# Queries and keys moved in two parts by Pool and SP, two products for each differential map, and the bias in two transfers: a two-layer encoder on one NeuronCore

## The chip, the core and the metric

The kernel runs on one core of one Trainium2 chip. The metric is the device time of one execution in microseconds (us). The kernel before takes 1178.91 us, the median of 3 runs (1178.65 to 1179.13).

## The reference, cut to what matters

The input x is 256 tokens by 2048, float32. Two layers follow each other; each is a norm, one input projection, attention in several head groups, a gate, one output projection, a norm and the residual.

```python
# layer 0: w_in is 2048 x 8192
h = rms_norm(x, pre_g)
qa, ka, va, ga, qb, kb, vb, gb = split(h @ w_in)
oa = neighbourhood_attention(qa, ka, va, rpb)   # 8 heads of 128, bias by distance in row and column
# B: 8 heads, each with two maps over 64 of the 128 rows of q and k
qb = partial_rope(qb.reshape(b, s, 8, 2, 64)); kb = partial_rope(kb.reshape(b, s, 8, 2, 64))
sc = einsum("bqhcd,bkhcd->bchqk", qb, kb) * 64 ** -0.5
p = softmax(sc)
ob = einsum("bhqk,bkhd->bqhd", p[:, 0] - lam * p[:, 1], vb)
x = x + rms_norm(concat(oa * silu(ga), rms_norm(ob) * 0.8 * silu(gb)) @ w_out, post_g)
# layer 1: w_in is 2048 x 12288: three dilated windows (8 heads each), merged by their
# denominators, and 8 query heads over 2 key heads with a sink; then the same gate, w_out and norm
```

## The kernel before, in words

**Every weight is used once**, so the kernel streams 196 chunks of 1 MB (four blocks of 128 rows by 512 columns). SP loads chunk n into one of 4 raw buffers (L354), ACT rounds it to float32r (`w_hi`, L760), DVE subtracts to get the rest (`w_lo`, L1054), and TensorE makes three products for each pair of block and token tile: hi by hi, lo by hi, hi by lo (L497). That is 24 products of 128 rows by 512 columns for a chunk. ACT and DVE prepare chunk s + 2 while TensorE is at chunk s; there are 3 split buffers.

**A body** is 12 chunks: four give 512 columns of queries (blk 0), four the keys (blk 1), four the values (blk 2). ACT takes a finished block out of PSUM into `unit` (L767), Pool applies the rotary turn to queries and keys (`rotate`, L440 to L447; none for kind A). The attention of a body's four heads (a unit) is worked into the next body: each engine's program calls `attention(u, h)` for the half chunks h = 0 to 23, `h = 2 s` and `2 s + 1`, in its own fixed order. The order on DVE in slot s is: `attention(2s)`, `attention(2s+1)`, the transposition of the next unit's queries and keys if s is 10 (`turn_qk`, L1096, two instructions), then `split_lo` for chunk s + 2. For kind D `attention(2s+1)` comes after `split_lo`. ACT has `attention(2s)`, `split_hi`, `attention(2s+1)`.

**Queries and keys need the head dimension on the partitions.** DVE transposes blocks of 32 x 32 into `postg` (`blocks`); then SP issues 16 moves of 64 KB (`gather`, L361), each with the query and the key part of one 32-partition group, into `qk_raw`. SP's queue carries the weight loads too, and the moves stand ahead of the load of the same slot. ACT and DVE split the result into hi and lo for kinds A, W, B and D (`split_qk_hi` at h = 2, `split_qk_lo` at h = 3).

**The units** are, in order: A, A, B, B in layer 0; W, W, G, G, G, G, D in layer 1. Layer 0 has 5 bodies, layer 1 has 8. Kind B are the differential heads. Its queries are split into `split_q`, where map 0 has rows 0 to 63 and map 1 rows 64 to 127, and Pool has set the other half to zero (L464); the keys are `k_hi` and `k_lo` over all 128 rows. A map of a head is then three products of 128 rows by 256 keys for each of two tiles (L629):

```python
for t in range(NT):
    for n, (a, b) in enumerate(PARTS):   # hi*hi, hi*lo, lo*hi
        m = nc.tensor.matmul(..., split_q[:, c, a, t * UH + j, :],
                             keys_of((k_hi[:, :, :], k_lo)[b], j), start=(n == 0), stop=(n == len(PARTS) - 1))
```

Kind D transposes its shared keys on TensorE at h = 4 (`turn_shared_k`, L580), after Pool's rotary turn of the third block, which is in the same slot as ACT's taking of it.

**The bias of kind A** is loaded by Pool in 32 transfers of 64 KB (L422) into `mix`, two for each head and tile, as runs of 64 elements; DVE adds the mask in the last four slots of the first body (L1452), one semaphore for each pair of heads.

Of the kernel before, what the change touches and what calls it, by code (L numbers as in the profile page):

```python
# [27 lines left out]
P = 128  # L28
# [16 lines left out]
TURN = 10  # L45
QK_DMAS = 16 * QUADS * QUADS
# [5 lines left out]
RPB_R, RPB_C = 15, 31  # L52
SCALE = HEAD ** -0.5
# [6 lines left out]
CREDITED = ("o_full", "o_taken", "probs_turned", "pt_ready", "probs_ready", "unit_done", "o_squared", "roped")  # L60
# [78 lines left out]
def build(nc, weights, x_turned, x_perm, consts, identity, pre_g, post_g, rpb, lam, subln, sink, out):  # L139
    with ExitStack() as ctx:  # L140
# [14 lines left out]
        with nc.sbuf_tensor("split_q", [P, 2, 2, NT * UH, P], F32R) as split_q:  # L155
            pass
# [28 lines left out]
        with nc.sbuf_tensor("q_lo", [P, 2, NT * UH, P], F32R) as q_lo:  # L185
# [16 lines left out]
        warm = sb("warm", [P, 1])  # L202
        std = sb("std", [P, NT])
# [33 lines left out]
        blocks = postg[:, :].rearrange("p (j b n) -> p j b n", j=QUADS, b=2)  # L237

        acc = [[ctx.enter_context(nc.psum_tensor(f"acc{s}_{t}", [P, NB], F32)) for t in range(NT)]
               for s in range(3)]  # L240
# [4 lines left out]
                 "x_hi first_hi first_lo warm_in ones_in row_sums row_full hi_ready lo_ready chunk_used tile_done proj_ready roped rope_a "  # L245
                 "mix_turned sp_moved1 sp_moved0 pool_moved1 pool_moved0 turn_full turn_hi turn_taken qk_turned qk_in qk_hi qk_ready k_full k_split k_ready g_ready "
# [4 lines left out]
                 "pre_sq pre_sum pre_var pre_std pre_rdy lam_p lam_s lam_e bias_rdy "  # L251
                 "y_sq y_scaled y_sum y_var y_std y_rdy "
                 "rs_v rs_s rs_rdy tanh_done gate_u gate_done q_zeroed").split()
# [6 lines left out]
        bias_in_two = [sem(f"bias_in_two{i}") for i in range(UH)]  # L260
# [47 lines left out]

        def split_units(u):

            return u.index - 4 if u.kind == "D" else u.index
# [19 lines left out]
        def _(sp):  # L331
# [44 lines left out]
            for layer in range(2):  # L376
# [3 lines left out]
                for u, b, i in loops(sp, layer):  # L380
                    for s in range(BODY):
                        if u is not None and u.by_blocks:
                            for h in (2 * s, 2 * s + 1):
                                for j in u.stages(h, 2):
                                    move_probs(u, j)
                        if s == TURN and turned_next(layer, u) is not None:
                            gather(turned_next(layer, u))
                        load(CHUNK0[layer] + BODY * b + s + 2 + RAW, i)
# [14 lines left out]
        def _(pool):  # L403
# [11 lines left out]
            for h in range(8):  # L415
                for t in range(NT):
                    for half in range(2):
                        r = 2 * t + half
                        src = bass.AP(rpb.tensor, h * RPB_R * RPB_C + (7 - r) * RPB_C + 15 - (GRID_W - 1),
                                      [[1, GRID_W], [RPB_C, ROWS], [1, GRID_W]])  # L420
                        at = (h * NT + t) * SEQ
                        pool.dma_start(bias_in[half * 64:half * 64 + 64, at:at + SEQ].rearrange(  # L422
                            "p (j k) -> p j k", j=ROWS), src).then_inc(bias_in_two[h // 2], 16)
# [24 lines left out]

            pool.wait_ge(S["consts_in"], 16)
            for layer in range(2):  # L450
                for u, _, _ in loops(pool, layer):
                    if u is None or u.kind == "A":
                        continue
                    turns = ((0, NB), (1, NB), (2, 2 * HEAD)) if u.kind == "D" else ((0, NB), (1, NB))
                    for k, (blk, cols) in enumerate(turns):
# [5 lines left out]
                    if layer == 0 and u.index == 2:  # L461

                        pool.wait_ge(S["masked"], 2 * UH)
                        pool.memset(split_q[:, :, :, :, :].rearrange("p c b a n -> p (c b a n)").bitcast(F32), 0.0).then_inc(  # L464
                            S["q_zeroed"], 1)
                if layer == 0:

                    pool.wait_ge(S["qk_in"], QK_DMAS * UNITS[0])
# [13 lines left out]
        def _(pe):  # L482
# [268 lines left out]
        def _(act):  # L751
# [49 lines left out]
            def split_qk_hi(u):  # L801

                act.wait_ge(S["qk_in"], QK_DMAS * u.index + QK_DMAS)
                if u.kind == "B":

                    act.wait_ge(S["q_zeroed"], 1)
# [11 lines left out]
                else:  # L818
                    nc.scalar.activation(k_hi[:, :, :], qk_raw[:, :, 1, :], ACT.Copy).then_inc(S["qk_hi"], 1)
# [11 lines left out]
            def attention(u, h):  # L831
# [5 lines left out]
                if h == 2:  # L837
                    split_qk_hi(u)
                if h == 4 and u.kind == "D":
# [105 lines left out]
            for layer in range(2):  # L945
# [4 lines left out]
                for u, b, i in loops(act, layer):  # L950
                    for s in range(BODY):
# [3 lines left out]
                        if s in takes:  # L955
# [7 lines left out]
                            if u is not None and s > 0:  # L963

                                act.wait_ge(S["qk_turned"], u.index + 1)
# [82 lines left out]
        def _(dve):  # L1048
# [39 lines left out]
            def turn_qk(layer, index):  # L1088

                if layer == 0 and index < 2:  # L1090

                    dve.wait_ge(S["proj_ready"], PROJ0[0] + 3 * index + 2)
                else:
                    dve.wait_ge(S["roped"], CREDIT + 2 * (index - 2) + 2)
                for blk in range(2):
                    m = nc.vector.transpose(blocks[:, :, blk, :].rearrange("p j (n c) -> p j n c", c=QUAD),  # L1096
                                            unit[:, blk, :, :].rearrange("p t (h j c) -> p j (t h) c", j=QUADS, c=QUAD))
                m.then_inc(S["qk_turned"], 1)

            def split_qk_lo(u):  # L1100

                for blk in range(2):

                    dve.wait_ge(S["qk_hi"], 2 * split_units(u) + blk + 1)
                    if u.kind == "B" and blk == 0:
                        for c in range(2):
                            rows = slice(64 * c, 64 * c + 64)
                            m = nc.vector.tensor_tensor(by_quads(split_q[rows, c, 1, :, :]), raw_quads(0, rows),
                                                        by_quads(split_q[rows, c, 0, :, :].bitcast(F32)), ALU.subtract)
                    elif blk == 0 or u.kind == "D":  # L1110
# [150 lines left out]
            def attention(u, h):  # L1261
                if u is None:
                    return
                if h == 3 and u.kind != "G":
                    split_qk_lo(u)
                if h == 4 and u.kind == "D":
# [136 lines left out]
            for layer in range(2):  # L1403
# [5 lines left out]
                for u, b, i in loops(dve, layer):  # L1409
                    for s in range(BODY):  # L1410
# [25 lines left out]
                        if s == TURN and turned_next(layer, u) is not None:  # L1436
                            turn_qk(layer, turned_next(layer, u))
# [152 lines left out]
```

## Time and profile before

| | |
|---|---|
| median of 3 runs | 1178.91 us (1178.65 to 1179.13) |
| the profiled execution, device time | 1178.83 us |
| its span, first to last instruction | 1176.6 us |
| mean granted TensorE clock | 0.998 |
| TensorE products busy | 1163.8 us, 99% of the span, 5476 products |
| DVE, ACT, Pool busy | 736.4, 583.8, 121.0 us |
| moved by DMA | 245.23 MB, 208 GB/s in the mean |

The profiled execution takes 2.2 us more than its span, for what lies around the first and the last instruction. It is 0.08 us below the median. A product's own duration in the profile is modelled and overlaps with the next one, so its cost is read from the distance between starts, or from a chain of many products.

### The profile page before, as it was taken

Reading aid. Unit: us, or ns where it says so; the run is one execution under the profiler, and the core shown is the slowest. Engines: PE = TensorE matmul, PEld = TensorE weight load, DVE = VectorE, ACT = ScalarE, POOL = GpSimd, SP = SyncE. Lnnn points to the kernel's source line nnn. Section 1 sums busy time; section 2 is a strip of 40 time slices with the busy share of each in tenths; the row PEclk is TensorE's granted clock in tenths of the full one; section 3 lists DMA queues with packets and bytes.
Section 4 is the critical chain, followed back from the end, with each engine's and each line's share of the span. In section 5 each row is a group of like instructions: output and inputs, shape, how many; then the busy total and the mean of one; then the engine's idle time right before and its main releaser. Section 6 shows DMA issues by size and latency. Waiting matters only on the chain.

```text
span 1176.6 us, 14665 instructions
## 1 busy us (share of the span) xinstructions
PE 1163.8 (99%) x5476; PEld 972.6 (83%) x5476; DVE 736.4 (63%) x842; ACT 583.8 (50%) x745; POOL 121.0 (10%) x177
## 2 busy tenths in 40 slices
PE   8999999999999999999999999999999999999997
PEld 6888888888888888888888888888888888888886
DVE  6676566656764975764666555565746667668654
ACT  6554445544555654564545454445444444446442
POOL 2400002000000310010100101102011002002100
PEclk9999999999999999999999999999999999999999
DMA  9987666744646785455767666666765766455741
GB/s 355 242 238 251 215 227 211 232 170 152 249 148 248 176 267 184 153 205 179 248 209 228 220 201 230 207 222 197 253 201 170 249 188 228 143 182 179 258 152 72
DMA packets 86441, 245.23 MB, mean 208 GB/s; under 512 B 33729, under 2 KB 51521, under 8 KB 60913
## 3 DMA queue, kind: packets, MB, share of 16 engines
q1 hardware_dynamic: 82704, 235.44, 60.2%
q0 software_dynamic: 3392, 8.96, 2.9%
q8 instruction: 36, 0.59, 0.2%
q14 instruction: 21, 0.16, 0.0%
q10 hardware_dynamic: 288, 0.08, 0.0%
HBM read 221.37 MB, written 8.39 MB: 195 GB/s over the span
## 4 chain that ended last, share of the span: by engine, by line
PE 96%; DVE 2%; ACT 1%; DMA 1%; issue 0%; SPq 0%; DVEq 0%; ACTq 0%
PE acc L497 89%; PE bank_x L660 2%; PE bank_y L613 1%; DMA raw<-weights 1%; PE bank_x L656 1%; PE bank_y L602 1%; PE bank_x L644 1%; DVE w_lo L1054 1%; PE bank_y L629 0%; PE bank_x L629 0%; PE bank_y L609 0%; DVE mix L1310 0%; ACT w_hi L760 0%; DVE resid L1365 0%; DVE probs L1301 0%
## 5 line engine op out<-in xcount | busy, mean ns | idle before, releaser
L497 PE MATMUL acc<-w_hi,act_hi 128*128 128x512 f32 x1560 | 615.8, 395 | 3.8 <-DVE w_lo L1054 3.8
L497 PE MATMUL acc<-w_lo,act_hi 128*128 128x512 f32 x1560 | 608.7, 390 | 0.0
L1054 DVE TENSOR_TENSOR w_lo<-raw,w_hi 128x2048 fp32r<-128x2048 f32 x195 | 449.0, 2305 | 180.6 <-ACT w_hi L760 180.4
L760 ACT ACTIVATE w_hi<-raw 128x2048 fp32r<-128x2048 f32 x195 | 373.5, 1916 | 298.7 <-PE acc L497 282.3
L497 PE MATMUL acc<-w_hi,act_lo 128*128 128x512 f32 x1560 | 418.2, 390 | 0.0
L497 PEld LDWEIGHTS acc<-w_hi,act_hi 128*128 128x128 f32 x1560 | 293.4, 188 | 62.1 <-issue 3.5
L497 PEld LDWEIGHTS acc<-w_hi,act_lo 128*128 128x128 f32 x1560 | 293.3, 188 | 62.2 <-DVE act_lo L1072 0.4
L497 PEld LDWEIGHTS acc<-w_lo,act_hi 128*128 128x128 f32 x1560 | 293.5, 188 | 57.3
L767 ACT ACTIVATE unit<-acc,pre_r 128x512 f32<-128x512 f32 x78 | 49.4, 685 | 123.0 <-PE acc L497 119.8
L440 POOL TENSOR_TENSOR rope_c<-unit,cst 128x256 f32<-128x256 f32 (+1 forms) x19 | 14.1, 740 | 728.0 <-ACT unit L767 596.2
L1213 DVE TENSOR_SCALAR mix<-bank_x 128x256 f32<-128x256 f32 (+1 forms) x24 | 10.1, 421 | 65.8 <-PE bank_x L660 65.8
L782 ACT ACTIVATE probs<-scores,negm 128x256 f32<-128x256 f32 (+1 forms) x80 | 36.4, 458 | 29.7 <-DVE negm L1142 25.3
L1213 DVE TENSOR_SCALAR unit_out<-bank_x 128x256 f32<-128x256 f32 x16 | 6.8, 424 | 60.7 <-PE bank_x L656 60.7
L660 PEld LDWEIGHTS bank_x<-unit,pT 128*128 128x128 f32 x256 | 33.5, 191 | 2.5
L447 POOL TENSOR_TENSOR unit<-rope_c,rope_s 128x256 f32<-128x256 f32 (+1 forms) x19 | 34.9, 1838 | 1.5
L326 POOL DMA_DIRECT2D mix_raw<-mix_blocks x48 | 25.6, 541 | 84.0 <-DVE mix_blocks L1321 83.8
L660 PE MATMUL bank_x<-unit,pT 128*128 128x128 f32 x256 | 33.7, 274 | 0.0
L1096 DVE STREAM_TRANSPOSE postg<-unit 128x1024 f32<-128x1024 f32 x22 | 26.0, 1219 | 0.0
L991 ACT ACTIVATE probs<-acc 128x512 f32<-128x512 f32 x16 | 9.5, 595 | 32.5 <-PE acc L497 32.5
L1139 DVE TENSOR_REDUCE rmax<-scores 128x2 f32<-128x512 f32 (+1 forms) x40 | 23.2, 580 | 1.4
L1337 DVE TENSOR_TENSOR mix<-acc,postg 128x512 f32<-128x512 f32 x16 | 10.5, 687 | 19.6 <-ACT probs L991 19.6
L827 ACT ACTIVATE pT<-probs 128x512 f32<-128x512 f32 (+1 forms) x32 | 16.6, 518 | 9.7 <-DMA probs<-p_moved 9.6
(179 smaller groups left out, 619.6 us busy)
## 6 DMA issues: line engine op xcount, KB each, us to landing
raw<-weights SPq DMA_DIRECT2D x195, 1024.0 KB, 5.0
qk_raw<-postg SPq DMA_DIRECT2D x176, 64.0 KB, 2.1
p_moved<-p_blocks SPq DMA_DIRECT2D x16, 256.0 KB, 5.5
probs<-p_moved SPq DMA_DIRECT2D x64, 64.0 KB, 1.9
mix<-rpb POOLq DMA_DIRECT2D x32, 64.0 KB, 22.4
postg<-post_g POOLq DMA_DIRECT2D x2, 1024.0 KB, 8.0
resid<-x_perm POOLq DMA_DIRECT2D x2, 1024.0 KB, 8.6
p_moved<-p_blocks SPq DMA_DIRECT2D x16, 128.0 KB, 5.0
```

The source lines that it names most:

```text
L326: eng.dma_start(dst, mix_blocks[a * QUAD:(a + 1) * QUAD, c % 2, q, :, :, :]).then_inc(S[f"{done}{c % 2}"], 16)
L447: pool.tensor_tensor(v[whole], rc, rs, ALU.add).then_inc(S["roped"], 1)
L497: m = nc.tensor.matmul(tiles[t][:, :], a[:, kt, t * P:(t + 1) * P], w[:, buf, kk * NB:(kk + 1) * NB], start=(kt == 0 and a is act_hi and w ...
L660: m = nc.tensor.matmul(X[:, t * P:(t + 1) * P], pT[:, (t * NT + k) * P:(t * NT + k + 1) * P], unit[:, 2, k, col:col + HEAD], start=(k == 0 ...
L760: nc.scalar.activation(w_hi[:, at % SPLIT, :], raw[:, at % RAW, :], ACT.Copy).then_inc(S["hi_ready"], 1)
L767: m = nc.scalar.activation(dst[:, t, :], acc[blk][t][:, :], ACT.Copy, scale=pre_r[:, t:t + 1])
L782: m = nc.scalar.activation(probs[:, j % 2, t * w:(t + 1) * w], scores[:, j % 2, t * w:(t + 1) * w], ACT.Exp, bias=negm[:, 2 * j + t:2 * j ...
L827: nc.scalar.activation(pT[:, 0:n * P].rearrange("p (n a c) -> p a n c", a=QUADS, c=QUAD), probs[:, j % 2, 0:n * P].rearrange("p (a n c) -> ...
L1054: nc.vector.tensor_tensor(w_lo[:, at % SPLIT, :], raw[:, at % RAW, :], w_hi[:, at % SPLIT, :].bitcast(F32), ALU.subtract).then_inc(S["lo_r ...
L1096: m = nc.vector.transpose(blocks[:, :, blk, :].rearrange("p j (n c) -> p j n c", c=QUAD), unit[:, blk, :, :].rearrange("p t (h j c) -> p j ...
L1139: nc.vector.reduce_max(rmax[:, two], dst.rearrange("p (t n) -> p t n", t=NT), AX_X).then_inc(S["maxed"], 1)
L1213: nc.vector.tensor_scalar(dst, src, 1.0, None, ALU.mult).then_inc(S["o_taken"], 1)
```

## The change

Five edits go together.

- The queries of the next unit are transposed by DVE at slot 6 and the keys at slot 10 (8 and 10 in a layer's first body), one instruction each. Pool moves the queries in 16 DMAs of 32 KB as soon as they are transposed, and half of the keys in 8; SP moves the other half in 8. Before each group Pool does one sum of a column (`tick`).
- A differential map is two products for each tile. For map c the stationary operand holds the hi part of the queries in its own 64 rows and the lo part in the other 64; the moving operand `both_k[:, c, 0]` holds the hi part of the keys in both halves. One product of 128 rows is then hi*hi plus lo*hi. The second, hi*lo, is over the map's own 64 rows only (rows 0 to 63 for map 0, 64 to 127 for map 1).
- For this ACT makes six copies of 64 rows for a B unit, and DVE four differences of 64 rows; the semaphore is counted per map. Pool's filling with zeros is gone.
- The bias comes in two DMAs with runs of 219 elements; the DVE sum reads it through a strided, reversed access pattern.
- ACT's splitting of B and D is called at h = 1 and no longer at h = 2; DVE's for B at h = 2 and 3, for D at h = 2; D's transposition of the shared keys on TensorE, and what follows it on ACT and DVE, at h = 3.

```diff
-TURN = 10
-QK_DMAS = 16 * QUADS * QUADS
+TURNS = (6, 10)
+FIRST_TURNS = (8, 10)
+PART_DMAS = 16 * QUADS * QUADS
+HALF_DMAS = PART_DMAS // 2
...
-            def gather(index):
-
-                sp.wait_ge(S["qk_turned"], index + 1)
-                for a in range(QUADS):
+            def gather_keys(index):
+
+                sp.wait_ge(S["k_turned"], index + 1)
+                for a in (0, 1):
                     for j in range(QUADS):
-                        sp.dma_start(qk_raw[j * QUAD:(j + 1) * QUAD, a, :, :], blocks[a * QUAD:(a + 1) * QUAD, j, :, :]).then_inc(
-                            S["qk_in"], 16)
+                        sp.dma_start(qk_raw[j * QUAD:(j + 1) * QUAD, a, 1, :], blocks[1][a * QUAD:(a + 1) * QUAD, j, :]).then_inc(
+                            S["k_in_sp"], 16)
...
-            for h in range(8):
-                for t in range(NT):
-                    for half in range(2):
-                        r = 2 * t + half
-                        src = bass.AP(rpb.tensor, h * RPB_R * RPB_C + (7 - r) * RPB_C + 15 - (GRID_W - 1),
-                                      [[1, GRID_W], [RPB_C, ROWS], [1, GRID_W]])
...
+            for half in range(2):
+
+                src = bass.AP(rpb.tensor, (7 - 2 - half) * RPB_C + 15 - (GRID_W - 1),
+                              [[1, GRID_W], [RPB_R * RPB_C, 8], [1, BIAS_RUN]])
+                pool.dma_start(bias_in[half * 64:half * 64 + 64, 0:8 * BIAS_RUN].rearrange("p (h n) -> p h n", h=8),
+                               src).then_inc(S["bias_in"], 16)
...
+            def gather(index, blk):
+
+                pool.wait_ge(S[("q", "k")[blk] + "_turned"], index + 1)
+                pool.wait_ge(S["ticked"], CREDIT + 2 * index + blk)
+                pool.tensor_tensor(tick[:, :], cst[:, 0:1], cst[:, 1:2], ALU.add).then_inc(S["ticked"], 1)
+                for a in (range(QUADS), (2, 3))[blk]:
+                    for j in range(QUADS):
+                        pool.dma_start(qk_raw[j * QUAD:(j + 1) * QUAD, a, blk, :], blocks[blk][a * QUAD:(a + 1) * QUAD, j, :]).then_inc(
+                            S[("q", "k")[blk] + "_in"], 16)
...
-                    if layer == 0 and u.index == 2:
-
-                        pool.wait_ge(S["masked"], 2 * UH)
-                        pool.memset(split_q[:, :, :, :, :].rearrange("p c b a n -> p (c b a n)").bitcast(F32), 0.0).then_inc(
-                            S["q_zeroed"], 1)
+                        if blk < 2:
+                            gather(u.index, blk)
...
             def score_map(u, j, c):
+                pe.wait_ge(S["qk_ready"], 2 * split_units(u) + c + 1)
                 if c == 0:
-                    pe.wait_ge(S["qk_ready"], 2 * split_units(u) + 2)
...
                 for t in range(NT):
-                    for n, (a, b) in enumerate(PARTS):
+                    for part, rows in enumerate((slice(0, P), slice(64 * c, 64 * c + 64))):
                         m = nc.tensor.matmul((Y, X)[c][:, t * SEQ:(t + 1) * SEQ].rearrange("p (t a c) -> p t a c", t=NT, a=QUADS),
-                                             split_q[:, c, a, t * UH + j, :],
-                                             keys_of((k_hi[:, :, :], k_lo)[b], j), start=(n == 0), stop=(n == len(PARTS) - 1))
+                                             q_hi[rows, c, t * UH + j, :], keys_of(both_k[rows, c, part, :, :], j),
+                                             start=(part == 0), stop=(part == 1))
...
-                if u.kind == "D" and h == 4:
+                if u.kind == "D" and h == 3:
                     turn_shared_k(u)
...
             def split_qk_hi(u):
...
                     for c in range(2):
-                        rows = slice(64 * c, 64 * c + 64)
-                        m = nc.scalar.activation(by_quads(split_q[rows, c, 0, :, :]), raw_quads(0, rows), ACT.Copy)
-                    m.then_inc(S["qk_hi"], 1)
+                        mine, other = (slice(64 * r, 64 * r + 64) for r in (c, 1 - c))
+                        nc.scalar.activation(by_quads(q_hi[mine, c, :, :]), raw_quads(0, mine), ACT.Copy).then_inc(S["qk_hi"], 1)
+                        nc.scalar.activation(both_k[other, c, 0, :, :], qk_raw[mine, :, 1, :], ACT.Copy)
+                        nc.scalar.activation(both_k[mine, c, 0, :, :], qk_raw[mine, :, 1, :], ACT.Copy).then_inc(S["qk_hi"], 1)
+                    return
...
+            def split_both_lo(u, c):
+
+                mine, other = (slice(64 * r, 64 * r + 64) for r in (c, 1 - c))
+                dve.wait_ge(S["qk_hi"], hi_count(u) + 2 * c + 1)
+                nc.vector.tensor_tensor(by_quads(q_hi[other, c, :, :]), raw_quads(0, mine),
+                                        by_quads(q_hi[mine, c, :, :].bitcast(F32)), ALU.subtract)
+                dve.wait_ge(S["qk_hi"], hi_count(u) + 2 * c + 2)
+                nc.vector.tensor_tensor(both_k[mine, c, 1, :, :], qk_raw[mine, :, 1, :],
+                                        both_k[mine, c, 0, :, :].bitcast(F32), ALU.subtract).then_inc(S["qk_ready"], 1)
...
-                if h == 3 and u.kind != "G":
+                if u.kind == "B" and h in (2, 3):
+                    split_both_lo(u, h - 2)
+                if h == (2 if u.kind == "D" else 3) and u.kind not in ("B", "G"):
                     split_qk_lo(u)
```

## Rows read from the trace of the kernel before

**Rows 1.** The page: busy time of the engines, and the chain that ended last.

```profile
PE 1163.8 (99%) x5476; PEld 972.6 (83%) x5476; DVE 736.4 (63%) x842; ACT 583.8 (50%) x745; POOL 121.0 (10%) x177
PE 96%; DVE 2%; ACT 1%; DMA 1%; issue 0%; SPq 0%; DVEq 0%; ACTq 0%
```

**Rows 2.** Waits of TensorE: line, releaser, us in total, times, longest.

```profile
PE acc L497 <- DVE w_lo L1054: 3.8, 2, 3.1
PE bank_x L539 <- DVE pT L1390: 1.1, 1, 1.1
```

**Rows 3.** Products of L629 into bank y with the low keys: duration min/median/max, first and last start.

```profile
L629 PE MATMUL bank_y<-qk_low,split_q x16: 282/283/290, 236.7 to 355.1; 128*128 128x256 f32 x16
```

**Rows 4.** The chain in order of time, four of its pieces: start us, us.

```profile
236.73 0.72 PE bank_y L629 x6
...
249.63 0.89 PE bank_x L660 x8
...
251.24 2.73 PE acc L497 x12
...
330.75 0.72 PE bank_x L629 x6
```

**Rows 5.** Timeline of TensorE at two places: start us, us [idle before].

```profile
249.47 1.05 PE L660 MATMUL bank_x<-unit,pT 128*128 128x128 f32 x8
250.27 0.37 PE L629 MATMUL bank_y<-k_hi,split_q 128*128 128x256 f32 x1
250.48 0.28 PE L629 MATMUL bank_y<-qk_low,split_q 128*128 128x256 f32 x1
...
392.88 1.07 PE L497 MATMUL acc<-w_hi,act_lo 128*128 128x512 f32 x4
394.59 0.50 PE L497 MATMUL acc<-w_hi,act_hi 128*128 128x512 f32 x1 [0.64 <-DVE w_lo L1054]
394.93 0.39 PE L497 MATMUL acc<-w_lo,act_hi 128*128 128x512 f32 x1
```

**Rows 6.** DMA instructions by line: duration on the issuing queue, ns min/median/max.

```profile
L326 POOL DMA_DIRECT2D mix_raw<-mix_blocks x48: 496/550/622, 392.7 to 1097.6; - x48
DMA to landing us min/median/max: 1.7/4.9/6.6
...
L361 SPq DMA_DIRECT2D qk_raw<-postg x176: 507/591/1352, 72.6 to 977.5; - x176
L422 POOL DMA_DIRECT2D mix<-rpb x32: 622/692/770, 23.8 to 42.7; - x32
```

**Rows 7.** Timeline of ACT, DVE, TensorE around the second B unit's splitting.

```profile
292.88 2.36 DVE L1096 STREAM_TRANSPOSE postg<-unit 128x1024 f32<-128x1024 f32 x2
301.18 1.91 ACT L760 ACTIVATE w_hi<-raw 128x2048 fp32r<-128x2048 f32 x1
306.72 2.14 ACT L809 ACTIVATE split_q<-qk_raw 64x1024 fp32r<-64x1024 f32 x2 [3.63 <-DMA qk_raw<-postg]
309.85 3.71 ACT L760 ACTIVATE w_hi<-raw 128x2048 fp32r<-128x2048 f32 x2
312.52 2.28 DVE L1054 TENSOR_TENSOR w_lo<-raw,w_hi 128x2048 fp32r<-128x2048 f32 x1
317.57 0.40 PE L497 MATMUL acc<-w_hi,act_hi 128*128 128x512 f32 x1
```

**Rows 8.** Timeline of Pool, DVE and TensorE at the start of unit D.

```profile
979.97 2.37 POOL L443 TENSOR_TENSOR rope_s<-unit,cst 128x64 f32<-128x64 f32 x1
982.42 2.39 POOL L447 TENSOR_TENSOR unit<-rope_c,rope_s 128x128 f32<-128x128 f32 x1
979.75 7.21 DVE L1054 TENSOR_TENSOR w_lo<-raw,w_hi 128x2048 fp32r<-128x2048 f32 x3
985.19 0.39 PE L497 MATMUL acc<-w_hi,act_hi 128*128 128x512 f32 x1
```

**Rows 9.** Timeline of DVE in the first body: the first sum of the bias.

```profile
64.02 1.42 DVE L1452 TENSOR_TENSOR resid<-mix,cst 128x256 f32<-128x256 f32 x4
```

More of the change, by code:

```diff
@@ L154, in build @@
         mix = sb("mix", [P, NT, D_MODEL])
-        with nc.sbuf_tensor("split_q", [P, 2, 2, NT * UH, P], F32R) as split_q:
+        with nc.sbuf_tensor("both_k", [P, 2, 2, QUADS, NT * UH * QUAD], F32R) as both_k:
             pass
@@ L202, in build @@
         warm = sb("warm", [P, 1])
+        tick = sb("tick", [P, 1])
         std = sb("std", [P, NT])
@@ L259, in build @@
         landed = [sem(f"landed{i}") for i in range(RAW)]
-        bias_in_two = [sem(f"bias_in_two{i}") for i in range(UH)]
         def const(name):
@@ L307, in in_token_order, with hi_count @@
             return src, dst[:, c * CK + k, :].rearrange("p (n b r) -> p n b r", n=4, b=4)
+        def hi_count(u):
+            return 2 * split_units(u) + (0 if u.kind == "A" else 2 * (u.index - 2) if u.kind == "B" else 4)
         def split_units(u):
@@ L385, in _ @@
                                     move_probs(u, j)
-                        if s == TURN and turned_next(layer, u) is not None:
-                            gather(turned_next(layer, u))
+                        if s == TURNS[1] and turned_next(layer, u) is not None:
+                            gather_keys(turned_next(layer, u))
                         load(CHUNK0[layer] + BODY * b + s + 2 + RAW, i)
@@ L836, in attention @@
                         order_pT(u, j)
-                if h == 2:
+                if h == (1 if u.kind in ("B", "D") else 2):
                     split_qk_hi(u)
-                if h == 4 and u.kind == "D":
+                if h == 3 and u.kind == "D":
                     act.wait_ge(S["k_full"], 1)
@@ L1100, in split_qk_lo @@
[L1100 to L1110, printed above, removed]
+                    dve.wait_ge(S["roped"], CREDIT + 2 * (index - 2) + 1 + blk)
@@ new lines, in turn_part @@
+                nc.vector.transpose(blocks[blk][:, :, :].rearrange("p j (n c) -> p j n c", c=QUAD),
+                                    unit[:, blk, :, :].rearrange("p t (h j c) -> p j (t h) c", j=QUADS, c=QUAD)).then_inc(
+                    S[("q", "k")[blk] + "_turned"], 1)
+            def split_both_lo(u, c):
[6 more added lines that the diff above has]
+                                        both_k[mine, c, 0, :, :].bitcast(F32), ALU.subtract).then_inc(S["qk_ready"], 1)
@@ L1111, in split_qk_lo @@
+            def split_qk_lo(u):
+                dve.wait_ge(S["k_in"], HALF_DMAS * u.index + HALF_DMAS)
+                dve.wait_ge(S["k_in_sp"], HALF_DMAS * u.index + HALF_DMAS)
+                for blk in range(2):
+                    dve.wait_ge(S["qk_hi"], hi_count(u) + blk + 1)
+                    if blk == 0 or u.kind == "D":
                         m = nc.vector.tensor_tensor(by_quads(q_lo[:, blk, :, :]), raw_quads(blk),
@@ L1263, in attention @@
                     return
-                if h == 3 and u.kind != "G":
+                if u.kind == "B" and h in (2, 3):
+                    split_both_lo(u, h - 2)
+                if h == (2 if u.kind == "D" else 3) and u.kind not in ("B", "G"):
                     split_qk_lo(u)
-                if h == 4 and u.kind == "D":
+                if h == 3 and u.kind == "D":
                     dve.wait_ge(S["k_split"], 1)
@@ L1435, in _ @@
                             turned(16 * layer + 2 * s + 2, layer)
-                        if s == TURN and turned_next(layer, u) is not None:
-                            turn_qk(layer, turned_next(layer, u))
+                        at = FIRST_TURNS if u is None else TURNS
+                        if s in at and turned_next(layer, u) is not None:
+                            turn_part(layer, turned_next(layer, u), at.index(s))
                         split_lo(CHUNK0[layer] + BODY * b + s + 2, i)
```

58 lines of the change are left out of this document (32 added, 26 removed).

## The prediction

> **What bounds the kernel now.** I read the page first: products fill 99% of the span, and the chain that ended last runs for 96% through TensorE [rows 1]. Then the waits of TensorE: it stood for 3.8 us behind `w_lo` (3.1 us of it near the start, 0.64 us at 394.59 us), and for 1.1 us behind its very first operand [rows 2, 5]. So nothing in the middle is late but one chunk. What is saved on ACT, DVE, Pool or a queue is worth nothing while this holds; what is saved on TensorE is worth all of it, as long as `w_lo` still comes in time.
>
> A product's own duration (0.283 us for a differential one [rows 3]) is no price, since products overlap. The chain gives the price: 6 differential products of a map take 0.72 us, at its first map as at its last, 0.120 us each [rows 4]. There are 8 heads of two maps, 16 maps, 96 products, 11.5 us.
>
> **The change part by part.**
>
> *Two products for three.* A map has 4 products in place of 6. The two that go are of the same shape as the rest: 2 x 0.120 = 0.24 us a map, 16 x 0.24 = 3.84 us in all. All of it is on the path.
>
> *The product over 64 rows.* No row of before shows one. At the low end it takes nothing, being hidden in its neighbour: 32 more slots of 0.120 us, another 3.84 us gained. At the high end TensorE stands empty each time it goes between 128 and 64 rows. Within a map the order is 128, 64, 128, 64 and then 128 again, 4 transitions a map, 64 in all. The price of an empty engine is in the trace. After 392.88 us four products follow each other and the next should start 4 x 0.227 = 0.91 us later (twelve take 2.73 us [rows 4]), at 393.79; its operand was late, and it started at 394.59, then took 0.34 us to its successor and not 0.227 us [rows 5]. The first product's surplus of 0.11 us is what a start on an empty array costs. To run empty costs what a product is in flight beyond its slot, 0.283 - 0.120 = 0.163 us [rows 3, 4]. Together 0.27 us a transition at the worst, 64 x 0.27 = 17.5 us. The nearest rows are other changes of the kind of product. Eight value products of 128 columns in full float32 stand between float32r products. From 249.47 us they and the first differential product take 1.01 us until 250.48 [rows 5]; eight at 0.111 us (0.89 us in the chain [rows 4]) and one at 0.120 us make 1.01 us. Changing the kind is free within the 0.01 us the trace resolves. I take 0.006 us a transition, half of that, 0.4 us in all, and a full slot of 0.120 us for the product over 64 rows, since its 256 columns are the same and I know of no row in which fewer rows shorten it.
>
> The Trainium skill (TensorEngine Tiling, Key Properties) speaks against this: changing the tiling mode, and not just the tile, drains TensorE, and it counts 64 rows as a mode of its own. By the Trainium skill (TensorE: Matmul & The Clock Gate, Part 2, step 4) a drain is some 128 cycles, an estimate of 0.053 us at 2.4 GHz; 64 of them are 3.4 us, and the sum would be 1178.4 us.
>
> *Splitting on ACT and DVE.* For a B unit ACT had 3 copies and now has 6, each 1.07 us whether over 64 rows or 128 [rows 7], 3.2 us more, twice. They stand at the same place of its order as before (nothing lies between h = 1 and h = 2 there). DVE goes from 3 to 4 differences of some 1.2 us. Neither is on the path; the cover is the lead of `w_lo`. In the second B unit it is thinnest: `w_lo` of the fourth chunk was done at 312.52 + 2.28 = 314.80 us and TensorE wanted it at 317.57 us, 2.8 us of lead [rows 7]. ACT had then waited 3.6 us for the moves.
>
> *The moves.* In that unit DVE could transpose only at 292.88 us [rows 7]. Now the queries are long gone by then (slot 6) and the keys need one instruction, to 294.1 us. Pool's `tick` may be held by DVE's `w_lo`: beside DVE's row of three, two of Pool's small sums ran 2.37 and 2.39 us and ended with DVE's instructions [rows 8]. That is up to 296.4 us. Eight DMAs of 0.55 us on Pool end at 300.8 us; landing takes 4.9 us, at the most 6.6 us [rows 6]: 305.7 to 307.4 us. SP's eight at 0.59 us are out by 299 us, 4.7 us earlier than its 16 were, so the weight loads behind them gain. ACT is free at 303.1 us, so its wait is 2.6 to 4.3 us; six copies end at 312.1 to 313.8 us, `w_hi` 1.9 us and `w_lo` 2.3 us later, 316.3 to 318.0 us. Against 317.57 us this is a lead of 1.3 us or a stall of 0.4 us. I take no stall. Elsewhere Pool has 16 x 0.55 = 8.8 us for the queries between slots 6 and 8 (two slots are 11 us), and SP is relieved; the other thin place, the chunk at 394.59 us [rows 5], hangs on the end of the last head and moves along with TensorE. DVE's two transpositions are only apart, not more.
>
> *D's shared keys* move from h = 4 to h = 3, that is to the half chunk that starts at 985.19 us. Pool's rotary turn ends at 982.42 + 2.39 = 984.81 us [rows 8], so 0.4 us are left. Nothing is gained by coming earlier. If Pool slips by one of DVE's instructions, TensorE stands up to 2 us.
>
> *The bias, the zeros.* 32 DMAs of 0.69 us become two with fewer, longer runs; the first use is at 64.02 us, the issue was over by 43.4 us [rows 6, 9]. Pool's filling goes too. Pool and DMA have room in both places and TensorE waits for neither: 0. It costs nothing while both transfers land in the 39 us from 25 to 64 us; DVE now needs both at once.
>
> **The sum**, against the profiled execution's 1178.83 us (span 1176.6 and 2.2 us around it): 1178.83 - 3.84 + 0.4 = 1175.4 us. That execution is 0.08 us under the median of the three runs, which I leave in the rounding. A change of over 0.2% (2.4 us) is about what a measurement can tell from none, so the forecast, -0.3%, is little beyond it.
>
> **The rivals.**
>
> *A, the forecast:* a transition costs up to 0.02 us; 1175.0 to 1176.4 us. For it: changing the kind of product is free [rows 5]. Against it: those all use the full height of the array.
>
> *B, a part of the gain is given back:* each transition costs 0.02 to 0.10 us, because the array empties in part. The break-even is 3.84 / 64 = 0.060 us. Middle: 64 x 0.055 = 3.5 us, 1178.5 us, no change that can be told. The drain that the Trainium skill (TensorEngine Tiling, Key Properties) names falls in here.
>
> *C, slower:* at each transition within `score_map` TensorE waits for the whole product in flight, 0.163 us or more, since the next weights can't be loaded under it. 64 x 0.163 = 10.4 us, 1185.4 us; with the surplus of an empty start 1192.5 us. It decides from 0.10 us a transition (6.2 us less 3.8 us is 2.4 us). For it: the row at 394.59 us shows that an emptied TensorE pays. Against it: there it had waited for data, not for itself.
>
> *D, late keys:* in the second B unit or at D's shared keys TensorE stands 0.4 to 2 us: 1175.8 to 1177.4 us. For it: leads of 1.3 and 0.4 us. Against: both hold by the rows.
>
> *E, the 64-row product is hidden in part:* down to 1171.5 us. Both products write the same sums one after the other, so I give it little.
>
> **How the numbers follow.** A 0.49, B 0.24, C 0.18, D 0.06, E 0.03. Faster by over 0.2% is A, E and a third of D, with rounding 0.53; within it B and the rest of D, 0.28; slower C and a little of B, 0.19. Predicted: 1175.4 us. A's own range is 1174.5 to 1176.4 us. The range reaches from 1174.5 us, where E begins and the spread of runs (0.25 us) is taken in, through B, whose end is 1181.2 us, to 1182.0 us; C's bulk and E are left out.
>
> **What would show it.** Right: 64 differential products, a map of four taking 0.48 us in the chain, the one over 64 rows with a start distance near 0.120 us, and the big product behind a map at its usual distance. The wait of TensorE for `w_lo` stays 3.8 us in total with no new line in its list; all 3.4 us are gained between 236 and 360 us and later stretches are as long as before. Wrong by B or C: distances of 0.14 us and more around the 64-row product, a map of 0.55 us or more. Wrong by D: a wait of TensorE on `w_lo` near 317 us or on Pool's line 447 near 985 us. The prediction is wrong if the gain comes from any stretch without B heads, or from the start.

## The result, and the profile after

The changed kernel is slower: 1187.84 us, the median of four runs (1186.87 to 1188.27), against 1179.02 us of the kernel before beside it (1178.65 to 1180.33), a ratio of 1.0074, 95% interval 1.0062 to 1.0087. The prediction was 1175.4 us, faster, and its range ended at 1182.0 us. The profiled execution took 1187.74 us, with a span of 1185.9 us and a granted clock of 0.995 (before: 0.998).

The page after, busy time of the engines:

```profile
PE 1172.6 (99%) x5444; PEld 972.1 (82%) x5444; DVE 740.4 (62%) x844; ACT 590.4 (50%) x751; POOL 254.1 (21%) x433
```

TensorE still sets everything (the chain that ended last runs for 96% through it, as in [rows 1]), with 32 products fewer and 8.8 us more of busy time. Nearly all of the 9.3 us by which the span grew are time in which the page shows TensorE busy. Waits of TensorE in the kernel after (columns as in [rows 2]):

```profile
PE acc L513 <- DVE w_lo L1076: 4.6, 2, 4.0
```

This is the wait of before, 0.8 us longer. The others are there in both kernels: 1.1 us at the very start, on `w_hi` 0.5 us (0.8 us before) and on `resid` 0.3 us. No wait on keys and none on Pool's turn has come. So the loss isn't a wait for another engine. The chain after, columns as in [rows 4]:

```profile
237.52 1.06 PE bank_y L645 x4
238.58 2.92 PE acc L513 x12
...
367.08 1.06 PE bank_x L645 x4
```

Four differential products take 1.06 us where six took 0.72 us [rows 4], and the twelve big ones behind a map 2.92 us where twelve take 2.73 us. It is the same at the first head and at the last. The groups of TensorE after, one row for each shape (columns: busy us, mean ns of one | idle before):

```profile
L645 PE MATMUL bank_y<-both_k,q_hi 64*128 64x256 f32 x16 | 6.1, 383 | 0.0
L645 PE MATMUL bank_y<-both_k,q_hi 128*128 128x256 f32 x16 | 5.8, 364 | 0.0
L645 PE MATMUL bank_x<-both_k,q_hi 128*128 128x256 f32 x16 | 5.3, 334 | 0.0
```

The records of the products over half the rows are 0.1 us longer than that of a full one was (0.283 us, [rows 3]), and those of the full ones next to them 0.05 to 0.08 us longer. The place is narrow enough to see single starts. TensorE and its weight loads (PEld) at the first map after:

```profile
237.36 1.22 PE L645 MATMUL bank_y<-both_k,q_hi 128*128 128x256 f32 x4
238.51 0.50 PE L513 MATMUL acc<-w_hi,act_hi 128*128 128x512 f32 x1
238.85 0.39 PE L513 MATMUL acc<-w_lo,act_hi 128*128 128x512 f32 x1
```

```profile
237.14 0.19 PEld L645 LDWEIGHTS bank_y<-both_k,q_hi 128*128 128x128 f32 x1
237.57 0.81 PEld L645 LDWEIGHTS bank_y<-both_k,q_hi 64*128 64x128 f32 x3 [0.25 <-issue]
```

The first product of the map starts at 237.36 us. The load of the second one's weights, over 64 rows, starts only at 237.57 us, 0.21 us later, and PEld had stood for 0.25 us with nothing that the profile names to wait for. A slot of 256 columns is 0.120 us [rows 4], so the load starts 0.09 us after the slot was over, and 0.07 us before the (modelled) end of that product's record. The record of the second product begins together with its load and is 0.10 us longer than usual (0.383 us, above); the third follows 0.31 us behind it. So a change of height (a step, from here on) costs some 0.09 us in front of the first product of the new height and some 0.10 us behind its start. The starts in the map are 237.36, 237.57, 237.88 and 238.20 us, the big product's is 238.51 us: 0.21 us, then three times 0.31 us, and 0.34 us instead of 0.227 us to the second big one.

**Where the 9 us arose.** Counting by the starts of the weight chunks, the same chunk starts 0.79 us later than before at 24 us. Each head of B then adds 1.0 to 1.1 us (its two maps together), 8.6 us over the eight heads, and from 376 us to the end the difference stays at 9.4 us. TensorE in stretches (us, busy (instructions), granted clock, DMA share, GB/s), first before, then after:

```profile
236.00:376.00 140.00, 140.00 (x710) 1.00 0.54 195
376.00:1169.00 793.00, 792.10 (x3702) 1.00 0.61 200
```

```profile
236.00:385.00 149.00, 149.00 (x679) 1.00 0.51 182
385.00:1179.00 794.00, 793.10 (x3705) 1.00 0.61 200
```

710 products less the 32 removed are 678; after needs 149 us for 679. The granted clock is 1.00 in both, and the stretch behind it is equal to 1 us in 793.

### The profile page after: what moved, and what is told of

It is laid out like the page before. It is cut to its first block, busy times and chain, and to the rows that moved or that the text cites. A ratio compares the mean times of both kernels' runs of the same rounds, so it can differ in the third digit from the quotient of the medians.

```text
span 1185.9 us, 14840 instructions
## 1 busy us (share of the span) xinstructions
PE 1172.6 (99%) x5444; PEld 972.1 (82%) x5444; DVE 740.4 (62%) x844; ACT 590.4 (50%) x751; POOL 254.1 (21%) x433
## 4 chain that ended last, share of the span: by engine, by line
PE 96%; DVE 2%; ACT 1%; DMA 1%; issue 0%; SPq 0%; DVEq 0%; ACTq 0%
PE acc L513 88%; PE bank_x L676 2%; PE bank_y L629 1%; PE bank_y L645 1%; PE bank_x L645 1%; PE bank_x L672 1%; PE bank_y L618 1%; DMA raw<-weights 1%; PE bank_x L660 1%; DVE w_lo L1076 1%; PE bank_y L625 0%; DVE mix L1340 0%; ACT w_hi L776 0%; DVE resid L1395 0%; DVE probs L1331 0%
## 5 line engine op out<-in xcount | busy, mean ns | idle before, releaser
L460 POOL DMA_DIRECT2D qk_raw<-postg x264 | 130.5, 502 | 5.7 <-issue 5.7
L457 POOL TENSOR_TENSOR tick<-cst 128x1 f32<-128x1 f32 x22 | 25.2, 1146 | 266.2 <-DVE postg L1117 232.2
```

Source lines behind the costliest of these rows:

```text
L457: pool.tensor_tensor(tick[:, :], cst[:, 0:1], cst[:, 1:2], ALU.add).then_inc(S["ticked"], 1)
L460: pool.dma_start(qk_raw[j * QUAD:(j + 1) * QUAD, a, blk, :], blocks[blk][a * QUAD:(a + 1) * QUAD, j, :]).then_inc(S[("q", "k")[blk] + "_in ...
```

## The experiments

The first four kernels separate three theories. One: a step between 128 and 64 rows costs about 0.19 us, four times a map (the theory of the steps, T in the expectations). Two: a product over 64 rows is slow in itself, whatever its neighbours (of the rows, S). Three: the new moves and copies hold TensorE up (of the moves, R). Each kernel starts from the one after, unless it says otherwise.

**Both products over all rows.** The half of the second operand that map 0 doesn't use is zeroed once by Pool, and the product takes all 128 rows.

```
- enumerate((slice(0, P), slice(64 * c, 64 * c + 64)))
+ enumerate((slice(0, P), slice(0, P)))
+ pool.wait_ge(S["masked"], 2 * UH)
+ pool.wait_ge(S["ticked"], CREDIT + 2 * u.index + 2)
+ pool.memset(both_k[:, :, 1, :, :] ..., 0.0).then_inc(S["q_zeroed"], 1)
+ act.wait_ge(S["q_zeroed"], 1)
```

> The changed kernel, but the second product of a map over all 128 rows; Pool fills the other half of its keys with zeros once. Theory T (going between 128 and 64 rows costs TensorE some 0.19 us each time, and nothing else in the change costs): no transitions are left, each of the 64 differential products is 0.12 us apart, a map has 0.48 us in the chain, the time is 1175 to 1176.5 us. Rival R (the changed kernel loses by what else is in it: the moves by Pool, more copies on ACT, the start): the time stays at 1184 us or more.

Measured: 1176.1 us (1175.1 to 1177.19, 11 runs), ratio to before 0.9979 (0.997 to 0.9988). TensorE at the same map, and its weight loads:

```profile
237.03 0.64 PE L650 MATMUL bank_y<-both_k,q_hi 128*128 128x256 f32 x4
...
237.74 0.39 PE L518 MATMUL acc<-w_lo,act_hi 128*128 128x512 f32 x1
```

```profile
237.03 0.43 PEld L650 LDWEIGHTS bank_y<-both_k,q_hi 128*128 128x128 f32 x3
237.39 0.19 PEld L518 LDWEIGHTS acc<-w_hi,act_hi 128*128 128x128 f32 x1
```

Four products now take 0.48 us, 0.120 us each, and every weight load starts beside the product in flight. From the map's first product to the second big one behind it: 0.71 us, after 1.49 us. That is 0.78 us for 4 steps, 0.195 us each. The moves, copies and splits are all still those of the changed kernel, so the theory of the moves falls: they aren't what loses 9 us. They aren't quite free either, as "Where the gain of the full rows went" shows.

**The order 128, 128, 64, 64.** The two loops change places: two steps a map instead of four, the same products.

```
- for t ...: for part, rows in enumerate(...):
+ for part, rows in enumerate(...): for t ...:
+ start=(part == 0 and t == 0), stop=(part == 1 and t == NT - 1)
```

> The changed kernel, but a map's four products in the order 128, 128, 64, 64 rows: two transitions a map in place of four. Theory T (the price is on the transition, 0.19 us): 32 fewer, 6.2 us less, 1181.7 us, and between the two products over 64 rows the starts are 0.12 us apart. Rival S (the price is on every product over 64 rows, and on the one behind it by its weights): the distance after each of the two stays at 0.31 us and the time near 1187.8 us.

Measured: 1180.9 us (1179.81 to 1181.89, 10 runs), ratio 1.0019 (1.001 to 1.0028).

```profile
235.80 0.83 PE L645 MATMUL bank_y<-both_k,q_hi 128*128 128x256 f32 x4
...
236.90 0.40 PE L513 MATMUL acc<-w_lo,act_hi 128*128 128x512 f32 x1
```

1.10 us over the same distance, 0.39 us above the full rows for two steps: 0.195 us each. The number of 64-row products is the same as in the changed kernel; were the product slow in itself, 1.49 us would have stayed. One expectation failed: the two products over 64 rows start 0.22 us apart (236.13 and 236.35 us) and not 0.12 us, since the second half of the step into 64 rows is paid behind the first of them.

**Before, with all six products over the map's own 64 rows.** This has 96 short products and two steps a map, into the run and out of it. The other half of the rows held zeros before, so leaving it out changes no sum.

```
+ rows = slice(64 * c, 64 * c + 64)
- split_q[:, c, ...], keys_of((k_hi[:, :, :], k_lo)[b], j)
+ split_q[rows, c, ...], keys_of((k_hi[:, :, :], k_lo)[b][rows], j)
```

> The kernel before, but all six products of a map over the map's own 64 rows: 96 products over 64 rows, two transitions a map, 32 in all. Theory T: 32 x 0.19 = 6.2 us more than the kernel before, 1185.2 us, and 0.12 us between starts inside a map. Rival S (every product over 64 rows takes 0.31 us): 96 x 0.19 = 18.5 us more, 1197.5 us.

Measured: 1185.53 us (1184.82 to 1185.78, 4 runs), ratio 1.0057 (1.0042 to 1.0072).

```profile
236.97 0.39 PE L497 MATMUL acc<-w_hi,act_lo 128*128 128x512 f32 x1
237.29 0.39 PE L630 MATMUL bank_y<-k_hi,split_q 64*128 64x256 f32 x1
237.51 0.28 PE L630 MATMUL bank_y<-qk_low,split_q 64*128 64x256 f32 x1
237.63 0.40 PE L630 MATMUL bank_y<-k_hi,split_q 64*128 64x256 f32 x2
237.87 0.28 PE L630 MATMUL bank_y<-qk_low,split_q 64*128 64x256 f32 x1
237.99 0.28 PE L630 MATMUL bank_y<-k_hi,split_q 64*128 64x256 f32 x1
...
238.53 0.40 PE L497 MATMUL acc<-w_lo,act_hi 128*128 128x512 f32 x1
```

Inside the run the short products start 0.12 us apart (237.51, 237.63, 237.87, 237.99), like full ones. That decides against the theory of the rows: the product isn't slow, the step is. One can see both steps of the map: into 64 rows, the last product of the old height takes 0.32 us to its successor (0.227 us is usual for 512 columns) and the first of the new height 0.22 us to its own (0.12 us is usual), 0.19 us more together. Out of 64 rows the same two surpluses stand again. For comparison the same map in the kernel before:

```profile
236.57 0.28 PE L629 MATMUL bank_y<-k_hi,split_q 128*128 128x256 f32 x1
...
237.52 0.39 PE L497 MATMUL acc<-w_lo,act_hi 128*128 128x512 f32 x1
```

Counted from the start of the big product before the map, it is 0.95 + 0.227 = 1.18 us there against 238.53 - 236.97 = 1.56 us here: 0.38 us for two steps. So the price is paid into 64 rows and out again, and with 512-column products on the other side too.

**The 64-row product first.** Its order is 64, 128, 64, 128, still four steps, now with the first behind a product of 512 columns. If a long product hid the step's work, this would be faster.

```
- for part, rows in enumerate((slice(0, P), slice(64 * c, 64 * c + 64))):
+ for part, rows in ((1, slice(64 * c, 64 * c + 64)), (0, slice(0, P))):
+ start=(part == 1), stop=(part == 0)
```

> The changed kernel, but within each tile the product over 64 rows comes first: 64, 128, 64, 128. There are four transitions a map as before, but the first of them now follows a product of 512 columns and not one of 256. Theory T with a price that does not depend on the product before (it is the way through the array): 1187.8 us. If the price is the loading of weights that can't be hidden under a short product, the long one hides it and the map costs up to 0.19 us less, 16 x 0.19 = 3.1 us less, 1184.7 us.

Measured: 1186.61 us (1186.03 to 1187.39, 4 runs), ratio 1.007 (1.0055 to 1.0086). It is the changed kernel's time (1186.77 us in its repeat below). In the chain, TensorE from the map's first product:

```profile
236.11 1.26 PE bank_y L645 x4
237.38 2.72 PE acc L513 x12
```

The map takes 1.26 us and the twelve behind it 2.72 us, together 3.98 us as after (1.06 + 2.92 us). Only the place of the last 0.2 us has moved. Nothing is hidden under 512 columns.

Averaged over all 16 maps, from the start of the last product before a map (a big one, in 6 of the 16 a product with the values) to that of the second big one behind it, the six kernels give:

| kernel | steps a map | products | us | over the row with its products and no step, per step |
|---|---|---|---|---|
| before | 0 | 6 | 1.139 | |
| all 64 rows | 2 | 6 | 1.526 | 0.193 |
| full rows | 0 | 4 | 0.898 | |
| grouped | 2 | 4 | 1.284 | 0.193 |
| after | 4 | 4 | 1.674 | 0.194 |
| 64 first | 4 | 4 | 1.674 | 0.194 |

**Where the gain of the full rows went.** By that table the maps give back 16 x 0.241 = 3.85 us, just the 3.84 us of the prediction, but the medians differ by some 2.8 us (0.9979 of 1178.9 is 1176.4, and 1176.1 was measured). By chunk starts in the profile, TensorE is 2.71 us earlier behind the eight heads than ahead of them. Two places took 0.27 us (273 us) and 0.54 us (322 us) back, and 0.33 us lie in a few ns here and there on the products of 512 columns. DVE at the first of them, then TensorE at the second, full rows:

```profile
265.74 1.24 DVE L1123 STREAM_TRANSPOSE postg<-unit 128x1024 f32<-128x1024 f32 x1
266.90 2.25 DVE L1082 TENSOR_TENSOR w_lo<-raw,w_hi 128x2048 fp32r<-128x2048 f32 x1
269.07 0.68 DVE L1184 TENSOR_REDUCE bmax<-bank_x 128x2 f32<-128x512 f32 x1
```

```profile
322.02 0.66 PE L665 MATMUL bank_x<-ident,probs 128*128 128x128 f32 x4 [0.33 <-DVE probs L1208]
```

At the first, the transposition of the queries now stands ahead of a `w_lo` and pushes the row maximum of the second map back; with maps this short the softmax comes too late by a little. The second is the place where ACT makes its six copies. Whether the slots mattered was tried by moving the two turns (slots 6 and 10 in the changed kernel and with full rows). First 7 and 10, full rows otherwise:

```
- TURNS = (6, 10)
+ TURNS = (7, 10)
```

> The kernel with full-height products (e1), but the queries are transposed in slot 7 and no longer in slot 6. e1 gained 3.7 us on the maps and gave back 0.8 us at two heads: 0.27 us near 273 us (fourth slot pair of the first B unit) and 0.54 us near 322 us (first head of the second). Theory T2 (in slot 6 DVE's transposition and the split behind it stand between the two maps of head 2, and TensorE then waits for the probabilities): the first of the two goes, the second stays, 0.27 us less than e1 in the trace; that is at the edge of what the times can tell. Rival (that wait comes from Pool's DMAs or from the shorter maps alone): both stay.

Measured: 1175.25 us (1173.64 to 1176.98, 11 runs), ratio 0.9972 (0.9963 to 0.9981). In the profile the loss at 273 us is gone, as expected. One of 0.23 us at 284 us has come, where Pool's rotary turn now falls together with DVE's softmax (see the last section), and that near 320 us stays at 0.51 us.

Then 7 and 9:

```
- TURNS = (6, 10)
+ TURNS = (7, 9)
```

> As e5, and the keys are transposed in slot 9, ahead of the last head's output, so that their moves land some 5 us earlier. Theory T3 (the 0.54 us near 322 us come from the keys of the second B unit landing at 304 us, which makes ACT late for the first head): this wait goes too, 0.8 us less than e1 in the trace. Rival (DVE now waits in slot 9 for Pool, which is still issuing the queries' moves before its rotary turn of the keys, and w_lo gets late): a new wait of TensorE for w_lo, no gain or a loss in the units from the second on.

Measured: 1175.97 us (1174.19 to 1176.96, 11 runs), ratio 0.9976 (0.9967 to 0.9985). The wait at 322 us is gone, as the theory that it comes from late keys expected. ACT's first copy of the second B unit at full rows, then ACT and DVE in the kernel with 7 and 9:

```profile
304.36 1.06 ACT L833 ACTIVATE q_hi<-qk_raw 64x1024 fp32r<-64x1024 f32 x1 [2.31 <-issue]
```

```profile
302.37 1.05 ACT L833 ACTIVATE q_hi<-qk_raw 64x1024 fp32r<-64x1024 f32 x1
```

```profile
313.43 0.69 DVE L1184 TENSOR_REDUCE bmax<-bank_y 128x2 f32<-128x512 f32 x1 [0.36 <-PE bank_y L650]
```

At full rows ACT waits 2.31 us for the keys, its six copies end at 310.82 us, and DVE is busy without a gap from the `w_lo` behind them (312.79 us) to the row maximum of the second map. With the keys a slot earlier ACT waits for nothing, that `w_lo` starts at 310.78 us, and DVE has 0.36 us to spare before the first maximum. So the 0.54 us come from the keys' landing and the copies behind it, by way of the softmax. But new losses have come, 0.22 us at 286 us and 0.79 us at 290 us. DVE in this kernel, then TensorE:

```profile
283.61 1.03 DVE L1200 TENSOR_SCALAR scores<-scores,binv 128x256 f32<-128x256 f32 x2
284.73 1.24 DVE L1208 SCALAR_TENSOR_TENSOR probs<-scores,bw 128x256 f32<-128x256 f32 x2
285.90 1.23 DVE L1123 STREAM_TRANSPOSE postg<-unit 128x1024 f32<-128x1024 f32 x1
287.06 2.25 DVE L1082 TENSOR_TENSOR w_lo<-raw,w_hi 128x2048 fp32r<-128x2048 f32 x1
289.23 0.68 DVE L1216 COPY pT<-bank_x 128x512 f32<-128x512 f32 x1
```

```profile
289.96 1.16 PE L681 MATMUL bank_x<-unit,pT 128*128 128x128 f32 x8 [0.52 <-DVE pT L1216]
```

The copy to `pT` stands behind the transposition of the keys and a `w_lo`, and TensorE waits 0.52 us for it. None of the three choices of slots removed the loss: it is 0.81 us (6 and 10), 0.74 us (7 and 10) and 1.01 us (7 and 9).

**Repeats beside these.** The full rows and the changed kernel, unaltered:

> e1 once more, beside e5 and e6 on their chip, as their baseline: 0.9979 of the kernel before with an interval of some 0.001, and the same two waits near 273 and 322 us (0.27 and 0.54 us) if they belong to the program; if they come from one run's DMA timing they differ.

> The changed kernel once more. Theory T: a map 0.53 us longer than before in every head, 8.5 us in the 16 maps, and 1187 to 1188.3 us; the distance at the start (chunk 2 began 0.8 us later than before in the first profile) is a matter of the run and not of the change, so it may come out at any value within a us.

Measured: 1175.96 us (10 runs), 0.9976 (0.9966 to 0.9985), with losses at the same two places, 0.27 and 0.66 us (TensorE waited 0.45 us at 322.31 us); and 1186.77 us (4 runs), 1.0069 (1.0053 to 1.0084). Both verdicts hold. The three choices of slots overlap in their intervals, and one kernel's loss differs by 0.12 us from profile to profile, so that 7 and 10 is the best is a hint and not shown.

**96 rows.** In the kernel with slots 7 and 10, map 0's second product goes over rows 0 to 95, map 1's over all. The rows left out are zeros.

```
- enumerate((slice(0, P), slice(0, P)))
+ enumerate((slice(0, P), slice(0, (96, P)[c])))
```

> e5, but the second product of map 0 over rows 0 to 95 (map 1's stays at 128), so map 0 goes between 128 and 96 rows as the changed kernel went between 128 and 64. If any other number of rows empties the array (theory T wide), the eight maps 0 cost 0.77 us more each, 6.2 us, 1181.5 us. If only a product that fits in half of the array does (theory T narrow), the distances in map 0 stay at 0.12 us and the time is that of e5, 1175.3 us.

Measured: 1175.77 us (1174.53 to 1176.86, 9 runs), ratio 0.9972 (0.9961 to 0.9982). TensorE, map 0, as above:

```profile
236.30 0.65 PE L650 MATMUL bank_y<-both_k,q_hi 128*128 128x256 f32 x4
...
237.02 0.40 PE L518 MATMUL acc<-w_lo,act_hi 128*128 128x512 f32 x1
```

0.72 us, against 0.71 us at full rows. A step between 128 and 96 rows is free within 0.01 us for a map of four; of the two heights tried only 64 rows, half the array's, pays.

Not tried: 32 rows, and a step from rows 0 to 63 to rows 64 to 127 without a change of height. What they cost is open.

## Why the prediction was wrong, step by step

**The step that failed** is the term "0.006 us a transition, 0.4 us in all". It was taken from the nearest row, a change between float32 and float32r products at full height [rows 5]. That row is about another thing: the format changes and the array's shape doesn't. Measured are 0.193 us, 12.4 us in all. With this one number the sum would be 1178.83 - 3.84 + 12.35 = 1187.3 us; the profiled execution took 1187.74 us. The 0.4 us between them are two things that the sum doesn't have: 0.8 us more at the start (last section), and 0.4 us less around the span (1187.74 - 1185.9 = 1.8 us, before 2.2 us). The second is there in every run of the kernels made from the changed one (1.8 us) and not in the one made from the kernel before (2.2 us); why is open. The prediction named the reason against its row itself (all its rows use the full height) and let the row decide.

**Rival C was the case.** It said that TensorE waits for the product in flight since the next weights can't be loaded under it, and the PEld rows show the load held back. It was priced 0.163 us without and 0.27 us with the start's surplus (0.163 + 0.11); 0.193 us lies between. The rows split it: the load starts 0.09 us beyond the slot of the product in flight (C: 0.163 us, to the end of its record, which the profile models), and 0.10 us more are lost behind it (C: 0.11 us). That these 0.10 us are the loading itself, which no product covers any more, fits the rows but wasn't tested alone. C had been given a chance of 0.18, and the range, cut at 1182.0 us, left out its whole priced span (1185.4 to 1192.5 us), which holds the result. **Rival B** needed a price near the break-even of 0.060 us; it was three times that.

The Trainium skill (TensorEngine Tiling, Key Properties) holds that changing the tiling mode drains TensorE, and the trace agrees: 0.193 us with each change between 64 rows and 128, none from 128 to 96. The drain estimated from the Trainium skill (TensorE: Matmul & The Clock Gate, Part 2, step 4), 0.053 us, is less than a third of a step, and the measurement decides: the estimate holds only the emptying. The Trainium skill (TensorE: Matmul & The Clock Gate, Part 2, step 1) has the next weights loaded while a product runs; the full-row kernel agrees (PEld at 237.03 us beside the products), and over a change of height the trace doesn't.

**The product count** was right: two products fewer a map are 1.139 - 0.898 = 0.241 us against 0.24 us, and they are on the path. **A full slot for the 64-row product** was right too (0.12 us between two of them), so rival E, that it is hidden in part, falls.

**The moves, the copies and the keys** (rival D) cost nothing in the changed kernel, as forecast, but in part by luck. The second B unit after:

```profile
299.28 2.15 POOL L457 TENSOR_TENSOR tick<-cst 128x1 f32<-128x1 f32 x1 [16.46 <-DVE postg L1117]
301.37 3.98 POOL L460 DMA_DIRECT2D qk_raw<-postg  x8
...
310.61 1.06 ACT L827 ACTIVATE q_hi<-qk_raw 64x1024 fp32r<-64x1024 f32 x1 [2.42 <-issue]
...
319.02 2.29 DVE L1076 TENSOR_TENSOR w_lo<-raw,w_hi 128x2048 fp32r<-128x2048 f32 x1 [0.72 <-ACT w_hi L776]
...
323.58 0.50 PE L513 MATMUL acc<-w_hi,act_hi 128*128 128x512 f32 x1
```

The small `tick` was held for 2.15 us beside DVE's `w_lo`, as feared from [rows 8]; a DMA cost Pool 0.50 us and not 0.55 us; ACT waited 2.4 us where 2.6 to 4.3 us were forecast; `w_lo` was done at 321.31 us and TensorE wanted it at 323.58 us. That is 2.3 us of lead (323.58 - 321.31) against a forecast of 1.3 us of lead to 0.4 us of stall. But part of this lead is the slower maps' own time. With the maps as short as forecast (full rows), the lead was 1.0 us (`w_lo` done at 315.08 us, wanted at 316.05 us), and the late keys with the six copies behind them did cost 0.54 us there: `w_lo` itself was in time, the softmax that DVE works off behind it wasn't. That is rival D by another wait, and the prediction didn't see it, since it asked only for `w_lo`'s lead. A slip in the same passage bears on nothing: SP's moves are out some 6 us earlier than before (299 us against 305.3 us), not 4.7 us. In D, Pool ended its turn at 994.19 us, TensorE started on it at 994.52 us and stood for nothing, as forecast. The bias in two DMAs cost nothing either: no wait on the bias appears among TensorE's.

## What to carry to other kernels

A product over half the rows is not cheaper than one over all, and each change between half and full height costs 0.19 us on TensorE, more than one 256-column product (0.12 us); both are measured here for float32r, behind 256 and 512 columns. Fill the unused rows with zeros and keep the full height, as here, 1176 instead of 1187 us; if short products can't be avoided, put them in one run. When a trace has no row for a change of the array's shape, a row in which only the type changes is no bound for it: the range has to hold the mechanism that the waits can't exclude. And where the bounding engine gets faster, ask of every engine that feeds it how much room it had, not only of the one with the thinnest lead.

## What the runs showed beyond the expectations

**The first wait differs from run to run, and the clock with it.** In the profiled executions TensorE stood for 3.1 to 4.4 us before the second chunk, and in ten of the eleven it then ran some products at half clock (5 to 11 starts lie 0.43 us apart; one in the kernel with 7 and 10). TensorE at the start of the changed kernel:

```profile
16.02 0.77 PE L513 MATMUL acc<-w_hi,act_hi 128*128 128x512 f32 x1 [3.95 <-DVE w_lo L1076]
16.58 0.63 PE L513 MATMUL acc<-w_lo,act_hi 128*128 128x512 f32 x1
17.00 0.63 PE L513 MATMUL acc<-w_hi,act_hi 128*128 128x512 f32 x1
...
22.79 0.39 PE L513 MATMUL acc<-w_hi,act_hi 128*128 128x512 f32 x1
23.02 0.40 PE L513 MATMUL acc<-w_lo,act_hi 128*128 128x512 f32 x1
```

The starts are 0.42 us apart at first (16.58 to 17.00), at 1.2 GHz, and 0.23 us in the end (22.79 to 23.02), at 2.4 GHz. The mean granted clock from 12 to 24 us was 0.72 after, at full rows (both runs) and all 64 rows, 1.00 with 7 and 10, and 0.86 in the other six. The third chunk began at 24.18 us in the changed kernel and at 23.16 us in its unaltered repeat, so this 1 us (and the 0.79 us above) is not the change's. The start alone moves a profile by up to 2.2 us here (the third chunk at 21.94 us with 7 and 10, at 24.18 us after), which is nearly what the full rows gain, so a gain of this size can't be read from two profiled times. What decides the length of the wait was not tried.

**Vector work beside Pool's is slower.** In the kernel with 7 and 9, while Pool ran its rotary turn (282.86 to 285.3 us), DVE's two scalings took 1.03 us in place of 0.61 us at full rows, and the two `probs` 1.24 us in place of 0.88 us: 0.8 us that no count of instructions has. With 7 and 10 it is the same (1.03 and 1.25 us), and in both TensorE loses 0.22 or 0.23 us right behind it. With the queries transposed in slot 6 Pool's turn comes earlier (it ends at 279.4 us) and misses DVE's softmax.
